# Two transformer blocks on one core: the sums of the norms taken tile by tile beside the products

## The chip, the cores and the metric

The kernel runs on one core of one Trainium2 chip. The metric is the device time of one execution in microseconds. The profile is one execution on the same core, recorded by the hardware profiler.

## The reference

512 tokens of width 2048 in fp32 go through two blocks. The first has a norm, a projection into a pooling half and a state-space half, an output projection and a gate; the second is an attention block with RoPE and 16 heads, and a gated feed-forward of width 5632, both modulated by a vector `c`.

```python
h = rmsnorm(x, norm_gain); proj = h @ w_in            # first block
h = x + concat([ya, yb]) @ w_out
h = h + (p @ w_ple) * sigmoid(h @ w_ple_gate)
x = rmsnorm(h, final_gain)                            # end of the first block

mod = silu(c) @ w_ada + b_ada                         # 6 x 2048 values
h = rmsnorm(x, g_pre_attn) * (1 + sc_a) + sh_a        # a norm of a norm
q, k, v = h @ w_in_2 ...                              # 16 heads
x = x + gt_a * rmsnorm(mix @ w_out_2, g_post_attn)
h = rmsnorm(x, g_pre_ffn) * (1 + sc_f) + sh_f
f = (silu(h @ w_gate) * (h @ w_up)) @ w_down
out = x + gt_f * rmsnorm(f, g_post_ffn)
```

A norm divides each token by the root of its mean square over 2048 channels plus 1e-6.

## The kernel before, in words

**Layout.** Activations lie with channels on the 128 partitions and the 512 tokens along the free axis: 16 tiles (`DT`) of 128x512. A projection is a sequence of *units*: one unit is 128 output channels, a weight of 128x2048 loaded by SyncE into `RAW[slot]`, two slots. fp32 precision comes from a split: ScalarE casts the weight to `WH` (`prep_hi`, L502 to L505), VectorE subtracts to get `WL` (`prep_lo`, L1085 to L1088), the activation is likewise `XH` and `XL`, and TensorE makes three products a tile (L816 to L818), so 48 a unit of 16 tiles. A unit waits for its `WL` (`lo_ready`), for each tile's `XL` (`x_ready`) and for its PSUM bank (`out_read`). The cast of the next weight waits for the unit before it.

**Order.** 32 input units with the scan between them, 8 GLU units, 16 output units (`U_OUT`), 2 of the small projection (`U_PLE`), 16 gate units (`U_PG`), 48 QKV units, three a head (`U_QKV`), 16 units of the second projection (`U_OUT2`), and 11 feed-forward chunks of 8 units gate/up and 4 units down (`U_FFN`).

**The vector c.** `mod` is taken on VectorE beside the output, gate, second projection and last feed-forward units: `ada_chunk` (L1104 to L1110) multiplies 1024 weights a partition with the row `CB` and sums. GpSimd loads the chunks into four slots (L352 to L359). `ada_row` (L687 to L692) on ScalarE waits until the chunks before are used, loads the row `CB` and applies Silu; it then goes on with the casts. `with_ada` (L1119) is VectorE's loop of such a unit: split of the next weight, ada chunks, evacuation.

**A norm** stands between two projections: `squares` on ScalarE (L507 to L510, four times 128x2048), `rms` on VectorE (L1095): four `tensor_reduce` (L1092), four products with a matrix of ones (`ones_sum`, L833 to L837) that put each token's sum on all partitions of PSUM bank 6, the root on ScalarE (L410), the reciprocal on VectorE (L1101), all 128x512. There are six:
- `rms(1)` ahead of the scan (not changed);
- `rms(2)` behind the gate: RES is scaled by it (L1497) and stored as x2; then RoPE's angles and tables and the lambda of the differential heads are computed (L1503 to L1524), and `rms(3)` of the result follows. `modulated` (L1525 to L1538) makes scaled tiles on VectorE, ScalarE adds the shift and casts (`modulated_hi`, L420 to L426), VectorE subtracts;
- `rms(4)` behind the second projection (evacuated to RES, L1667): scale (L1680), add to x2 (L1687), store as x3, `rms(5)` of the sum, `modulated`, and RES is filled with zeros (L1693) ahead of the feed-forward, which adds every chunk's outputs to it (L1727);
- `rms(6)` behind the last chunk, then scale, load of x3, add (L1740) and store (L802).

**Queues.** SyncE issues the weights and the scan's shuffles, GpSimd the ada chunks and spills, ScalarE x, p, `CB`, mask, positions, x2, x3 and the output. `CB`, the ada slots, RoPE's tables and the mask share 48 K to 62 K of each partition, so the tables and the mask come only after the ada chunks.

## Time and profile before

| | us |
|---|---|
| median of 3 runs | 3481.95 (3480.8 to 3482.26) |
| the profiled execution | 3481.74 |
| its span, first to last instruction | 3480.1 |
| TensorE busy | 3241.6 (93%) |
| VectorE busy | 1799.9 (52%) |
| ScalarE busy | 876.2 (25%) |
| TensorE's mean granted clock, 1 is full | 0.96 |

The span in 40 equal slices of 87 us; each digit is tenths:

```profile
PE   8999998999749999999798399999999999999995
DVE  7556565677774445655456823333333333333357
PEclk9999999999869999999699699999999999999997
```

A busy TensorE is not one at its peak: the records overlap, a product of 391 ns begins every 226 ns. "L1092" is a line of the kernel; a releaser in brackets is what ended an idle time.

### The profile page before, as it was taken

To read this page: it belongs to the slowest core of one execution; us is meant where nothing else is said; L and a number is where in the kernel's file an instruction comes from. 1 tells how busy PE (TensorE), PEld (TensorE's weight loads), DVE (VectorE), ACT (ScalarE), POOL (GpSimd) and SP (SyncE) were. 2 spreads that over 40 slices of the span, in tenths; PEclk is the share of its full clock that TensorE was granted. 3 is DMA by queue.
4 is the path that set the end of the run, shared out by engine and by line. 5 is a ranking of instruction groups with operands and counts; after the bars stand their busy time and mean duration, and the time that the engine had idled before them with its cause. 6 is when DMAs were issued, how large, how long until landed. Compare 5 with 4: busy or idle time off the path is not lost.

```text
span 3480.1 us, 37989 instructions
## 1 busy us (share of the span) xinstructions
PE 3241.6 (93%) x14672; PEld 2611.8 (75%) x14672; DVE 1799.9 (52%) x2225; ACT 876.2 (25%) x884; POOL 162.2 (5%) x307
## 2 busy tenths in 40 slices
PE   8999998999749999999798399999999999999995
PEld 6888877888528888887386188888888888888883
DVE  7556565677774445655456823333333333333357
ACT  4323332133332222322312311111111111111121
POOL 1111100111100000000011000000000000000010
PEclk9999999999869999999699699999999999999997
DMA  4443346757512122221265222222222222222263
GB/s 183 129 131 125 120 176 246 265 218 265 184 77 85 73 84 73 85 84 72 108 242 193 89 98 97 96 96 96 96 96 96 94 98 94 93 97 93 96 235 143
DMA packets 87927, 445.88 MB, mean 128 GB/s; under 512 B 18240, under 2 KB 18384, under 8 KB 51504
## 3 DMA queue, kind: packets, MB, share of 16 engines
q1 hardware_dynamic: 50336, 293.89, 23.9%
q0 software_dynamic: 34784, 121.03, 9.7%
q10 hardware_dynamic: 2736, 30.02, 2.1%
q8 instruction: 44, 0.72, 0.1%
q14 instruction: 27, 0.22, 0.0%
HBM read 417.36 MB, written 20.97 MB: 126 GB/s over the span
## 4 chain that ended last, share of the span: by engine, by line
PE 88%; DVE 8%; DMA 1%; ACT 1%; DVEq 1%; issue 1%; ACTq 0%; POOL 0%; SPq 0%; POOLq 0%
PE PS L816 27%; PE PS L818 27%; PE PS L817 27%; DVE SIG L1092 1%; PE PS L999 1%; PE PS L1023 1%; PE PS L1062 1%; DMA CB<-c_row_dram 1%; DVE TMP L1092 1%; DVE PART L1092 1%; DVE RES L1680 1%; DVE WL L1088 1%; DVE XL L1538 1%; PE PS L1014 1%; DVE RSTD L1101 0%
## 5 line engine op out<-in xcount | busy, mean ns | idle before, releaser
L816 PE MATMUL PS<-XH,WH 128*128 128x512 f32 x3488 | 1376.6, 395 | 68.5 <-DVE WL L1088 28.8
L817 PE MATMUL PS<-XL,WH 128*128 128x512 f32 x3488 | 1364.1, 391 | 0.0
L818 PE MATMUL PS<-XH,WL 128*128 128x512 f32 x3488 | 1364.0, 391 | 0.0
L1088 DVE TENSOR_TENSOR WL<-RAW,WH 128x2048 fp32r<-128x2048 f32 x270 | 618.2, 2290 | 588.8 <-ACT WH L505 588.4
L505 ACT ACTIVATE WH<-RAW 128x2048 fp32r<-128x2048 f32 x270 | 516.5, 1914 | 1454.6 <-PE PS L818 1452.4
L816 PEld LDWEIGHTS PS<-XH,WH 128*128 128x128 f32 x3488 | 658.7, 189 | 232.1 <-issue 71.4
L818 PEld LDWEIGHTS PS<-XH,WL 128*128 128x128 f32 x3488 | 658.8, 189 | 138.8
L817 PEld LDWEIGHTS PS<-XL,WH 128*128 128x128 f32 x3488 | 659.5, 189 | 136.0 <-issue 1.9
L816 PE MATMUL PS<-FH,WH 128*128 128x512 f32 x704 | 275.2, 391 | 2.2 <-DVE FL L1720 2.1
L817 PE MATMUL PS<-FL,WH 128*128 128x512 f32 x704 | 274.0, 389 | 0.0
L818 PE MATMUL PS<-FH,WL 128*128 128x512 f32 x704 | 273.9, 389 | 0.0
L1110 DVE CUSTOM_DVE_ANT_0 ADA<-ADA,CB 128x1024 f32<-128x1024 f32 x192 | 224.7, 1221 | 1.3 <-DMA ADA<-w_ada_dram 1.1
L1727 DVE TENSOR_TENSOR RES<-RES,PS 128x512 f32<-128x512 f32 x176 | 120.4, 686 | 199.6 <-PE PS L818 197.8
L359 POOL DMA_DIRECT2D ADA<-w_ada_dram x180 | 95.1, 529 | 1946.7 <-DVE MOD L1110 1679.1
L1716 DVE TENSOR_TENSOR FV<-PS,SIG 128x512 f32<-128x512 f32 x44 | 30.4, 692 | 266.6 <-PE PS L818 266.6
L816 PEld LDWEIGHTS PS<-FH,WH 128*128 128x128 f32 x704 | 132.1, 188 | 33.9 <-DVE FL L1720 6.8
L818 PEld LDWEIGHTS PS<-FH,WL 128*128 128x128 f32 x704 | 132.2, 188 | 27.6
L817 PEld LDWEIGHTS PS<-FL,WH 128*128 128x128 f32 x704 | 132.2, 188 | 27.1
L788 ACT ACTIVATE SIG<-PS 128x512 f32<-128x512 f32 x44 | 26.3, 599 | 382.2 <-PE PS L818 382.2
L837 PE MATMUL PS<-TMP,CON 128*128 128x512 f32 x12 | 11.4, 1049 | 92.9 <-DVE TMP L1092 92.9
L1552 DVE TENSOR_TENSOR TMP<-PS,ROPE 128x512 f32<-128x512 f32 x32 | 22.1, 692 | 121.5 <-PE PS L818 121.4
L837 PEld LDWEIGHTS PS<-TMP,CON 128*128 128x128 f32 x12 | 2.9, 290 | 97.4 <-DVE TMP L1092 97.3
(235 smaller groups left out, 1953.5 us busy)
## 6 DMA issues: line engine op xcount, KB each, us to landing
RAW<-w_units_dram SPq DMA_DIRECT2D x270, 1024.0 KB, 4.8
ADA<-w_ada_dram POOLq DMA_DIRECT2D x192, 512.0 KB, 5.6
BB<-x_dram ACTq DMA_DIRECT2D x2, 4096.0 KB, 12.2
spill_dram<-SIG POOLq DMA_DIRECT2D x24, 256.0 KB, 2.3
XV<-x_t_dram SPq DMA_DIRECT2D x4, 1024.0 KB, 11.0
BB<-x_t_dram ACTq DMA_DIRECT2D x1, 4096.0 KB, 12.3
x_dram<-RES ACTq DMA_DIRECT2D x1, 4096.0 KB, 11.1
x_dram<-BB ACTq DMA_DIRECT2D x1, 4096.0 KB, 12.1
```

Source lines behind the costliest of these rows:

```text
L359: gp.dma_start(ADA[slot][:, :], w_ada[bass.ds(first + ADA_SLOTS * (i + 1) + slot, 1)] .rearrange("a p n -> p (a n)")).then_inc(ada_loaded[ ...
L505: act.activation(WH[:, slot, :], RAW[:, slot, :], ACT.Copy).then_inc(hi_ready, 1)
L816: pe.matmul(PS[:, bank, :], wh, rh[:, x, :], start=k == 0, stop=False)
L817: pe.matmul(PS[:, bank, :], wh, rl[:, x, :], start=False, stop=False)
L818: ins = pe.matmul(PS[:, bank, :], wl, rh[:, x, :], start=False, stop=k == n - 1)
L999: ins = pe.matmul(PS[:, bank, c:c + w], QR[lo:hi, b * P:(b + 1) * P], KR[lo:hi, 0:w], start=True, stop=True, skip_group_check=True)
L1014: ins = pe.transpose(PS[:, TURN_BANK[b], k * P:(k + 1) * P], SMX[:, 0, BLK[b] + k * P:BLK[b] + (k + 1) * P], IDENT)
L1023: ins = pe.matmul(PS[:, 4, b * P:(b + 1) * P], VS[:, k, :], PT[:, c:c + P], start=k == 0, stop=k == b, skip_group_check=True)
L1088: v.tensor_tensor(WL[:, slot, :], RAW[:, slot, :], f32(WH[:, slot, :]), ALU.subtract)\
L1092: v.tensor_reduce(PARTS[c], src[:, 4 * c:4 * c + 4, :].rearrange("p t n -> p n t"), AX.X, ALU.add)\
L1110: v.tensor_tensor_reduce(ADA[slot][:, :], ADA[slot][:, :], CB[:, :], 1.0, 0.0, ALU.mult, ALU.add, (MODH if half else MOD)[:, t:t + 1]).the ...
L1727: v.tensor_tensor(RES[:, 4 * q + m, :], RES[:, 4 * q + m, :], PS[:, m, :], ALU.add).then_inc(out_read, 1)
```

## The change

1. `ada_row` is split in two: the load of `CB` and, later, `ada_silu`. The first load is issued in GLU unit 6, the second behind the last output unit, the third behind the last head's exponentials. The parts of `mod` are cut at 52 instead of 56 and the chunks are shared out differently.
2. RoPE's angles and tables and lambda are computed beside output units 1, 3, 5 and 7, in RES's free tiles, and stored to `rope_dram`; they are loaded with the mask behind the gate.
3. Behind the gate there is one reduction instead of two. Each gate tile is squared by ScalarE when it is final, and VectorE adds it, beside the units, into two sums, plain and weighted with final_gain^2 + eps. The scale of the norm of the norm is the root of (weighted mean + eps^2), so that RES itself stays unscaled; final_gain is folded into the modulation, and RES is scaled to x2 later, beside the second projection, with the row `R1ROW`.
4. The sum over partitions is taken with the squares as weights and a column of ones as the moving operand, so that each token's sum stands in a column [128 tokens, 4]; root and reciprocal run on that. A diagonal matrix times ones puts it back as a row in PSUM bank 7 (or 6), from which VectorE reads it.
5. The second projection is evacuated by ScalarE, scaled by gate and gain, and squared from PSUM; VectorE adds the squares. The next norm's squares are taken tile by tile. The last chunk is treated in the same way, with x3 loaded during it into XH's place; the outputs are stored in five parts.
6. The first two units behind the QKV and the feed-forward norm are interleaved tile by tile (`pair`), the second five tiles behind. RES is no longer filled with zeros: the first chunk copies.
7. ScalarE's loops over output and gate units are written out.

```diff
-ADA_OUT = ADA_PG = [4, 3] * 8
-ADA_OUT2 = [3] * 16
-ADA_FFN = [3, 3, 3, 3, 2, 2] * 2
+ADA_OUT, ADA_PG = [4, 3, 3, 3] * 4, [3, 3, 3, 4] * 4
+ADA_OUT2 = [4, 3] * 8
+ADA_FFN = [4] * 8 + [0] * 4
+LAG = 5
+STORES = [(0, 4), (4, 8), (8, 12), (12, 14), (14, 16)]
...
+        def token_scales(act, n, first=False):
+            act.wait_ge(ms_ready, n)
+            ins = act.activation(RC[:, 0:4], PS[:, 6, 0:4], ACT.Sqrt, bias=CON[:, C_EPS:C_EPS + 1], scale=1.0 / D)
+            if first:
+                ins = act.activation(RC[:, 4:8], PS[:, 6, 4:8], ACT.Sqrt, bias=EPS2, scale=1.0 / D)
+            ins.then_inc(sd_ready, 1)
...
+            for n in range(DT):
+                prep_hi((U_PG + n + 1) // 2, (n + 1) % 2)
+                if n >= 1:
+                    gate_square(n - 1)
+                act.wait_ge(out_done, O_PG + n + 1)
+                act.wait_ge(sig_used, 8 + n + 1)
+                act.activation(SIG[:, n % 2, :], PS[:, n % 2, :], ACT.Sigmoid).then_inc(sig_ready, 1)
+            act.activation(SPARE, ONES[:, 0:1], ACT.Sqrt)
+            gate_square(DT - 1)
+            prep_hi(U_QKV // 2, 1)
+            token_scales(act, 2, first=True)
...
+                act.activation(RES[:, n, :], PS[:, n % 2, :], ACT.Copy, scale=GATE[:, n:n + 1])
+                if n >= 2:
+                    act.wait_ge(acc_done, DT - 1 + n - 1)
+                act.activation(SIG[:, n % 2, :], PS[:, n % 2, :], ACT.Square).then_inc(out_read, 1)
+            prep_hi(U_FFN // 2, 1)
+            token_scales(act, 3)
...
+            def pair(n, o, x0):
+                for u in range(2):
+                    pe.wait_ge(out_read, READ0 + o + u - 1)
+                for k in range(TILES + LAG):
+                    for u, x in ((0, k), (1, k - LAG)):
+                        if not 0 <= x < TILES:
+                            continue
+                        if x == 0:
+                            pe.wait_ge(lo_ready, n + u + 1)
+                        if u == 0:
+                            pe.wait_ge(x_ready, x0 + x + 1)
...
+            def token_sums(src, col, weight, start, stop):
+                for b in range(4):
+                    ins = pe.matmul(PS[:, 6, col + b:col + b + 1], src[:, b * P:(b + 1) * P], weight,
+                                    start=start and b == 0, stop=stop, skip_group_check=True)
+                return ins
+            def token_rows(n, diag, bank):
+                pe.wait_ge(diag_ready, n)
+                pe.matmul(PS[:, bank, :], ONES, diag, start=True, stop=True).then_inc(row_ready, 1)
...
+            token_rows(3, TMP[:, :], 7)
+            for t in range(DT):
+                pe.wait_ge(sq_ready, 4 + DT + t + 1)
+                ins = token_sums(SQ[:, t, :], 0, ONES[:, 0:1], t == 0, t == DT - 1)
+            ins.then_inc(ms_ready, 1)
...
-            def rms(n, src):
+            def token_scales(n, cols=4):
                 v.wait_ge(sd_ready, n)
-                v.reciprocal(RSTD[:, :], RSTD[:, :])
+                v.reciprocal(RC[:, 0:cols], RC[:, 0:cols])
                 v.drain()
+                token_diag(TMP[:, :], cols - 4)
...
+            def gate_square_added(t):
+                v.wait_ge(sq_ready, 4 + t + 1)
...
+                v.tensor_tensor(BB[:, 0, :], BB[:, 0, :], BB[:, t, :], ALU.add)
+                v.scalar_tensor_tensor(out=ACC2[:, :], in0=BB[:, t, :], scalar=GF2[:, t:t + 1], in1=ACC2[:, :],
+                                       op0=ALU.mult, op1=ALU.add).then_inc(acc_done, 1)
...
-            rms(3, SQ)
-            modulated(RES, V_GPRE, DT, BB, 0, X_QKV)
+            token_scales(2, 8)
+            modulated(1, RES, BB, 0, X_QKV, U_QKV + 1)
+            token_diag(SIG[:, 0, :], 0)
...
+            token_scales(3)
+            v.wait_ge(row_ready, 3)
             for c in range(4):
                 sl = slice(4 * c, 4 * c + 4)
-                v.tensor_tensor(BB[:, sl, :], BB[:, sl, :], RES[:, sl, :], ALU.add)
-            v.drain().then_inc(src_ready, 1)
-            v.drain().then_inc(save_go, 1)
-            rms(5, SQ)
-            modulated(BB, V_GPF, 4 * DT, RES, 3 * DT, X_FFN)
-            v.drain()
-            v.memset(RES[:, :, :], 0.0)
+                row_scaled(PS[:, 7, :], sl)
+                v.tensor_tensor(BB[:, sl, :], BB[:, sl, :], RES[:, sl, :], ALU.add).then_inc(x3_ready, 1)
+            prep_lo(U_FFN + 1, 1)
+            token_scales(4)
+            modulated(4, BB, RES, 3 * DT, X_FFN, None)
```

In the first `modulated` the split of the second unit's weight stands between the tiles, behind the fourth scaled tile. `row_scaled` multiplies four tiles by the row in PSUM. The `Sqrt` on `SPARE` loads the root's table ahead of its use.

## Rows read from the trace of the kernel before

**Rows 1.** The page: busy time, share of the span and instructions by engine

```profile
PE 3241.6 (93%) x14672; PEld 2611.8 (75%) x14672; DVE 1799.9 (52%) x2225; ACT 876.2 (25%) x884; POOL 162.2 (5%) x307
```

**Rows 2.** Windows: length, busy (records) of PE, PEld, DVE, ACT, POOL; PEclk, DMA, GB/s

```profile
557.90:565.60 7.70, 0.10 (x1) 0.00 (x0) 2.48 (x2) 4.66 (x3) 0.00 (x0) 0.79 0.20 81
565.60:569.60 4.00, 3.94 (x10) 3.16 (x11) 4.00 (x7) 0.00 (x0) 0.53 (x1) 0.55 0.72 250
928.50:1011.10 82.60, 16.62 (x17) 4.01 (x16) 63.03 (x63) 26.21 (x23) 0.00 (x0) 0.52 0.13 52
1690.00:1700.00 10.00, 10.00 (x13) 3.53 (x12) 8.10 (x12) 3.75 (x6) 0.00 (x0) 0.50 0.00 0
1897.60:1967.80 70.20, 16.62 (x17) 4.04 (x17) 59.18 (x39) 19.26 (x14) 0.00 (x0) 0.52 0.10 45
3431.40:3480.10 48.70, 8.30 (x8) 2.00 (x8) 38.13 (x29) 9.28 (x6) 0.00 (x0) 0.52 0.42 172
```

**Rows 3.** Timeline from gate to QKV: start, us, engine, line, operation, count, idle before

```profile
928.12 0.39 PE L818 MATMUL PS<-XH,WL 128*128 128x512 f32 x1
930.11 0.69 DVE L1489 TENSOR_TENSOR RES<-RES,TMP 128x512 f32<-128x512 f32 x1
936.60 2.08 PE L837 MATMUL PS<-TMP,CON 128*128 128x512 f32 x2 [8.08 <-DVE TMP L1092]
1008.26 2.08 DVE L1533 SCALAR_TENSOR_TENSOR BB<-RES,SM,RSTD 128x512 f32<-128x512 f32 x3
1011.15 0.77 PE L816 MATMUL PS<-XH,WH 128*128 128x512 f32 x1 [7.70 <-DVE XL L1538]
1056.28 0.69 DVE L1632 COPY VT<-PS 128x512 f32<-128x512 f32 x1 [5.80 <-PE PS L818]
```

**Rows 4.** Timeline from the second projection to the third feed-forward unit

```profile
1897.23 0.39 PE L818 MATMUL PS<-XH,WL 128*128 128x512 f32 x1
1964.92 2.08 DVE L1533 SCALAR_TENSOR_TENSOR RES<-BB,SM,RSTD 128x512 f32<-128x512 f32 x3
2011.08 1.92 ACT L505 ACTIVATE WH<-RAW 128x2048 fp32r<-128x2048 f32 x1 [18.10 <-PE PS L818]
```

**Rows 5.** Timeline of VectorE behind the last product

```profile
3431.85 0.17 DVE L1115 TENSOR_TENSOR MOD<-MOD,MODH 128x16 f32<-128x16 f32 x1 [0.19 <-issue]
3465.94 8.90 DVE L1740 TENSOR_TENSOR BB<-BB,RES 128x2048 f32<-128x2048 f32 x4
```

**Rows 6.** Timeline in the second projection: units 1, 9 and 10 (unit's first waits)

```profile
1732.05 0.76 PE L816 MATMUL PS<-XH,WH 128*128 128x512 f32 x1 [7.84 <-DVE WL L1088]
1817.34 2.29 DVE L1088 TENSOR_TENSOR WL<-RAW,WH 128x2048 fp32r<-128x2048 f32 x1 [6.03 <-ACT WH L505]
1821.50 1.92 ACT L505 ACTIVATE WH<-RAW 128x2048 fp32r<-128x2048 f32 x1 [4.19 <-PE PS L818]
1832.38 1.92 ACT L505 ACTIVATE WH<-RAW 128x2048 fp32r<-128x2048 f32 x1 [8.96 <-PE PS L818]
```

**Rows 7.** Groups by form: out<-in, shape, count | busy us, mean ns | idle before

```profile
L885 PE MATMUL PS<-U,GT 128*128 128x64 f32 x128 | 15.1, 271 | 0.0
L885 PEld LDWEIGHTS PS<-U,GT 128*128 128x128 f32 x128 | 15.5, 191 | 0.6
L837 PEld LDWEIGHTS PS<-SIG,CON 128*128 128x128 f32 x24 | 5.8, 291 | 31.6 <-DVE SIG L1092 30.7 <-issue 1.0
L1110 DVE CUSTOM_DVE_ANT_0 ADA<-ADA,CB 128x1024 f32<-128x1024 f32 x192 | 224.7, 1221 | 1.3 <-DMA ADA<-w_ada_dram 1.1
L1533 DVE SCALAR_TENSOR_TENSOR BB<-RES,SM,RSTD 128x512 f32<-128x512 f32 x16 | 11.8, 747 | 0.1
L1658 DVE SCALAR_TENSOR_TENSOR BB<-BB,VEC,PS 128x512 f32<-128x512 f32 x8 | 6.0, 747 | 5.9 <-PE PS L1062 5.9
L498 ACT ACTIVATE SIG<-BB 128x512 f32<-128x512 f32 x16 | 9.9, 627 | 8.1 <-PE PS L1056 5.7 <-DVE BB L1612 2.4
L410 ACT ACT_TABLE_LOAD x5 | 6.4, 1283 | 0.1
```

## What I predict, and how

> **What bounds the kernel now.** I read the page first: TensorE is busy 93% of the span, VectorE 52% [rows 1]. So what can be won is TensorE's idle time, and the 40 slices and the chain of waits put nearly all of it where a norm ends. The windows view prices the stretches [rows 2]; its columns are length, busy time (records) of PE, PEld, DVE, ACT, POOL, the granted clock, DMA. Between the last gate product and the first QKV product lie 82.6 us in which TensorE has 17 records; between the second output projection and the feed-forward 70.2; after the last product 48.7; and 7.7 us ahead of the second output unit, where VectorE and ScalarE wait for the row `CB`. The clock falls to 0.50 (1.2 GHz) in each, and the restart shows it: 10 records in 4.0 us at 0.55, where full speed makes one in 0.2266 us.
>
> **The unit.** One unit of 48 products takes 10.88 us, the distance of two weight casts that wait for it [rows 6], so 0.2266 us a product and 0.68 a tile. VectorE's modulation has two instructions a tile; three first ones take 2.08 us [rows 3], so a pitch of 0.66 us, 1.325 a tile.
>
> **Part 1, the CB row.** It is now loaded during the unit before, so only its Silu, a cast and a split (some 6.5 us after the last GLU tile, at most 10.9 available) stand ahead of the second output unit. Goes: 7.7 us idle, and of the cold restart 4.0 us less 10 x 0.2266 = 1.7, together 9.4. The same at the second projection: 7.84 us idle [rows 6] and 1.7, less the load's issue of some 0.4 us that now stands ahead of the first head square: 9.1. Together **18.5**.
>
> **Part 2, gate to QKV.** Before: last product ends at 928.5, last residual add at 930.8, first modulation at 1008.26, first product 2.9 us later at 1011.1 [rows 2, 3], and the copy of V behind the third unit at 1056.28 [rows 3]. After, step by step from 928.5:
> - The last pass of VectorE is longer: four ada chunks instead of three (1.2 more), the two square additions (1.4), four small operations (0.25 each). These are 3.6 us; the pass used to wait some 1.5 us for the sigmoid, so the residual add ends 2.0 later, at 932.8. The 15 passes before hold 2.3 + 4.9 + 1.4 + 1.5 = 10.1 us at most of 10.88, so they stay covered.
> - ScalarE squares the last tile, 0.63 [rows 7]: 933.5. Its cast of the second QKV weight (1.92) runs beside the sums.
> - 8 sums with the last square, 16 records. No row has a product with one moving column. The nearest is 128x128 weights with 64 columns, records 271 ns long but overlapping: 128 of them are 15.1 us busy, 0.11 to 0.12 each, at full clock; a weight load there takes 191 ns, and 291 at the low clock [rows 7]. The difference, 0.1 us, is what 128 columns cost more at half clock, so I take 0.21 us a record there. I take the low clock here: 3.4 us, 936.9. The first 16 records lie ahead of the square.
> - Two roots on [128, 4] (some 0.25 each with the hand-over), reciprocal 0.2 (a 128x16 operation takes 0.17 [rows 5]), diagonal 0.69: 938.6. One row product at the low clock, 2.08 [rows 3]: 940.8. There the modulation starts: 67.5 us earlier.
> - The pair. First product 2.9 us later. VectorE has 32 steps of 0.66 and the split of the second weight, 2.29: tile 5 at +11.5, the last at +23.4. From tile 5 TensorE has both units: 11 x 1.36 + 5 x 0.68 = 18.3 us. That is slightly slower than VectorE's 1.325 a tile, so TensorE ends it at 940.8 + 11.5 + 18.3 = 970.6. Then the scale row (0.9) and the third unit; its cast and split wait for the first unit's end (966.5) and last 4.2 us, just covered. V at 971.5 + 10.9 = 982.4 against 1056.3: **73.8**.
> - Moved work: RoPE's angles and tables (21 operations on 128x512, each at most the 0.69 of V's copy [rows 3]) go beside output units 1, 3 and 5. Unit 3 gets ten, 6.9 us, and its pass takes 13.5 us, more than a unit, but each is followed by a lighter one, and the split that TensorE needs is first in each pass: no cost as long as that is so. The DMAs on ScalarE's queue (x2 4 MB, mask, RoPE) start at 937 and have 27 us before anybody reads.
>
> **Part 3, second projection to feed-forward.** Before: last product 1897.6, modulation 1964.92, third unit at 2010.9 [rows 4]. After:
> - Scaled copy, square (0.6 each) 1898.9; the weight cast 1.92 stands ahead of the root on ScalarE: 1900.8; root, reciprocal, diagonal 1.5; row 2.08: 1904.3.
> - Four times multiply (2.2), add (2.29), drain: 18.3, so 1922.6. It replaces 16 small multiplies and four adds.
> - The squares follow group by group; the 16 tiles give 128 records. At 0.21 us they take 27.3 us from 1909.9 on and end at 1937.2, later than VectorE. At 0.11 they keep up and end at 1927.1. Which clock TensorE has is the largest open question. The 16-row products between 1690 and 1700 keep it busy all the time and the clock stays at 0.50 [rows 2]; one moving column behind each weight load is nearer to that than to full products. I take 0.21.
> - Root to row 3.4 us: modulation at 1940.6. Pair: tile 5 at +9.3, end at 1968.2. Third unit: cast and split behind CB's load, its Silu and the SiLU of unit 0, some 1.5 us late: 1969.8. Against 2010.9: **41.1** (at 0.11: 51.5). The fill of RES with zeros (6.9 us) goes with it; the first chunk copies instead.
>
> **Part 4, the end.** Last add 3431.7 [rows 5]; square and its addition 0.8, 16 records of which 8 behind the last square (0.9 to 1.7), root to row 3.5: 3438.0. Then 8 operations on four tiles and four on two: 18.6, so 3456.6, where before the last add ends at 3474.8 [rows 5]. The last store is half as large: 5.3 us behind it before, some 4.9 after. **18.6**.
>
> **Part 5, what gets dearer.** Beside unit 7 of the second projection the split waits for CB; it ended at 1819.6, 1.8 us ahead of TensorE's need [rows 6]. Two more ScalarE operations and a later start take 2.5 us: 0.7 lost. The same wait in the last feed-forward chunk now falls at unit 3: 0 to 1.5. Together **-1.5**.
>
> **Sum.** 18.5 + 73.8 + 41.1 + 18.6 - 1.5 = 150.5. The profiled execution took 3481.7 us (span 3480.1 and 1.6 around it), within the three runs' spread round their median 3481.95. So 3331.
>
> **Where the Trainium skill bears on it.** TensorE: Matmul & The Clock Gate, section LDWEIGHTS, gives a load's time by its columns alone, 107 ns for 128, with no second value for the low clock. By that the sums would never lag, which is the first rival; the 291 against 191 ns of rows 7 speak against it. VectorE: DVE Perf Modes, the section on the TRN2 errata, gives an operand in PSUM 120 fixed cycles instead of 58, so an estimate of 65 ns more for each of the 41 operations that now read the row from PSUM, 2.7 us dearer in all. The rows disagree: with the row in PSUM 747 ns, with it in SBUF 747 [rows 7]. I take nothing.
>
> **Rivals.**
> 1. *The sums keep up* (0.25). TensorE takes 0.11 us a record, because loads of 128 rows count as work and the clock rises, or because they don't slow. For it: the loads do fill all 128 rows, unlike those at 1690, and full products bring the clock back in 4 us [rows 2]. 10.4 us less at part 3: 3320.5.
> 2. *Hand-overs are dearer* (0.17). If Square or the scaled copy needs another table than the root, each of three handovers has two table loads more, 6 x 1.28 = 7.7 [rows 7]; and 0.7 us more at each of six chains for small operations that the trace never shows. 3343. Against: behind the head norm's root, copies follow without a load.
> 3. *The clock stays low in a pair* (0.07). Every restart in rows 2 begins at half clock, and the first five tiles feed TensorE only half the time; the clock may come back late or drop once more. A whole pair at 1.2 GHz costs 16 us, both 33: 3347 to 3364.
> 4. *The pairing does nothing* (0.04): the second unit waits for the first, because its split comes late. 7.5 us each: 3346.
> 5. *VectorE becomes the bound* (0.02 in all, 0.01 of it slower than before). In 48 units (output, gate, second projection) it gets more work and every unit waits for its split or evacuation. Now a pass takes 9 to 13.5 us in a unit of 10.88. It costs 48 us for each us over; to eat 150 us the mean pass must reach 14.0 us. Counting instructions gives a mean of no more than 10.5, hence the low chance; at 11.5 it would be 3361.
>
> **How the numbers follow.** Forecast 0.45, the rivals as given. The forecast's own spread is 6 us. The range reaches from the sums that keep up with everything else a little cheaper, 3312, to the dearer hand-overs and one cold pair, 3352; outside lie less than 2 in 10. A difference under 0.2% (7 us) can't be told from none; faster 0.98, same 0.01, slower 0.01.
>
> **What would show it.** The pause from last gate product to first QKV product falls from 82.6 us to about 15; 70.2 becomes two pauses with 128 small records between, whose pitch (0.21 or 0.11) and clock decide rival 1; the tail falls from 48.7 to 30. No idle time of 7.7 us ahead of the second output unit. In the pairs records at 0.2266 and idle only in the first five tiles (rivals 3, 4). Output, gate and second projection: 174 us each, no TensorE idle (rival 5). Table loads between the last square and the root show rival 2. Wrong is the prediction if a chain holds a wait for a DMA, or if the gain goes to places not named here.

## The result, and the profile after

The changed kernel takes 3327.24 us (median of four runs, 3325.46 to 3327.49) where the kernel before takes 3481.38 (3479.53 to 3482.26): a ratio of 0.9557, 95% interval 0.954 to 0.9573. Forecast were 3331.0, with 3312 to 3352 as the range. The profiled execution took 3327.44 us with a span of 3325.8, so 154.3 us less than the span before.

The page of the changed kernel, its busy time by engine and TensorE and its granted clock in the 40 slices:

```profile
PE 3232.4 (97%) x14834; PEld 2634.6 (79%) x14834; DVE 1732.8 (52%) x2233; ACT 871.4 (26%) x948; POOL 162.3 (5%) x307
...
PE   8999999999989999998999999999999999999996
...
PEclk9999999999999999999798899999999999999998
```

TensorE's share of the span rose from 93% [rows 1] to 97% while its busy time hardly changed: the gain is idle time taken away. The slices that were 7 and 4, 3, and 5 in the kernel before are 8, 9 and 6 now. The windows view gives the stretches one by one, in the columns of rows 2: gate's last product to the first QKV product; that pair of units; the last product of the second projection to the first of the feed-forward pair; that pair; and the end.

```profile
918.98:931.40 12.42, 6.07 (x36) 4.36 (x35) 6.29 (x15) 6.97 (x10) 0.00 (x0) 0.72 0.50 211
931.40:958.80 27.40, 25.20 (x97) 19.18 (x98) 23.19 (x31) 11.33 (x14) 0.00 (x0) 0.88 0.42 163
1803.90:1849.60 45.70, 33.35 (x149) 30.01 (x147) 25.20 (x21) 14.19 (x24) 0.44 (x1) 0.55 0.41 159
1849.60:1874.80 25.20, 24.45 (x96) 18.54 (x96) 19.89 (x29) 14.16 (x17) 0.00 (x0) 0.93 0.08 21
3296.70:3325.80 29.10, 4.02 (x19) 2.36 (x18) 20.52 (x14) 1.51 (x3) 0.00 (x0) 0.56 0.35 144
```

82.6 us [rows 2] became 12.4; 70.2 became 45.7, of which TensorE is now busy 33.4, but with small records; 48.7 became 29.1. (The first and third windows open 0.2 us ahead of the last product's end. The last window of rows 2 opens 0.5 us behind it: the last product of the kernel before ends at 3430.94, so its tail is 49.2.) The chain of work behind the gate, from the timeline of the changed kernel (start, length, engine, line, operation, idle before):

```profile
921.43 0.69 DVE L1652 TENSOR_TENSOR RES<-RES,TMP 128x512 f32<-128x512 f32 x1
922.84 1.05 PE L912 MATMUL PS<-CON,BB 128*128 128x1 f32 x8 [1.93 <-ACT BB L749]
923.75 1.14 PE L912 MATMUL PS<-SM,BB 128*128 128x1 f32 x8
924.92 0.26 ACT L428 ACTIVATE SM<-PS,CON 128x4 f32<-128x4 f32 x1 [0.34 <-PE PS L912]
925.38 0.20 DVE L1214 RECIPROCAL SM<-SM 128x8 f32<-128x8 f32 x1 [3.26 <-ACT SM L430]
926.40 2.08 PE L919 MATMUL PS<-TMP,CON 128*128 128x512 f32 x2 [1.51 <-DVE TMP L1208]
928.51 2.06 DVE L1684 SCALAR_TENSOR_TENSOR BB<-RES,SM,PS 128x512 f32<-128x512 f32 x3 [2.17 <-PE PS L919]
931.39 0.76 PE L902 MATMUL PS<-XH,WH 128*128 128x512 f32 x1 [2.91 <-DVE XL L1691]
970.58 0.69 DVE L1794 COPY VT<-PS 128x512 f32<-128x512 f32 x1 [3.41 <-PE PS L865]
```

And the one stretch where TensorE is now late, between the second projection and the feed-forward:

```profile
1808.27 1.80 PE L919 MATMUL PS<-TMP,CON 128*128 128x512 f32 x2 [1.88 <-DVE TMP L1208]
1815.85 27.47 PE L912 MATMUL PS<-CON,SQ 128*128 128x1 f32 x128 [5.79 <-ACT SQ L802]
1828.85 2.19 ACT L802 ACTIVATE SQ<-BB 128x512 f32<-128x512 f32 x4 [2.37 <-DVE BB L1856]
1844.65 2.08 PE L919 MATMUL PS<-TMP,CON 128*128 128x512 f32 x2 [1.33 <-DVE TMP L1208]
1846.77 2.06 DVE L1684 SCALAR_TENSOR_TENSOR RES<-BB,SM,PS 128x512 f32<-128x512 f32 x3 [2.17 <-PE PS L919]
```

ScalarE has squared the last tile at 1831.04, and the 128 one-column records end at 1843.3: TensorE is 12.3 us behind its data.

### The profile page after: what moved, and what is told of

Same layout as the page of the kernel before. It is cut to its first block, busy times and chain, and to the rows that moved or that the text cites. A ratio compares the mean times of both kernels' runs of the same rounds, so it can differ in the third digit from the quotient of the medians.

```text
span 3325.8 us, 38222 instructions
## 1 busy us (share of the span) xinstructions
PE 3232.4 (97%) x14834; PEld 2634.6 (79%) x14834; DVE 1732.8 (52%) x2233; ACT 871.4 (26%) x948; POOL 162.3 (5%) x307
## 4 chain that ended last, share of the span: by engine, by line
PE 92%; DVE 5%; ACT 1%; DMA 1%; issue 1%; DVEq 1%; ACTq 0%; POOL 0%; SPq 0%; POOLq 0%
PE PS L863 28%; PE PS L865 28%; PE PS L864 28%; PE PS L1086 1%; PE PS L1110 1%; PE PS L912 1%; DVE WL L1199 1%; PE PS L1153 1%; ACT WH L519 1%; PE PS L1101 1%; PE PS L983 0%; PE PS L1147 0%; DMA CB<-c_row_dram 0%; PE PS L966 0%; PE PS L930 0%
## 5 line engine op out<-in xcount | busy, mean ns | idle before, releaser
L863 PE MATMUL PS<-XH,WH 128*128 128x512 f32 x3424 | 1344.5, 393 | 21.6 <-DVE XL L1450 14.3
L865 PE MATMUL PS<-XH,WL 128*128 128x512 f32 x3424 | 1334.8, 390 | 0.0
L864 PE MATMUL PS<-XL,WH 128*128 128x512 f32 x3424 | 1334.5, 390 | 0.0
L863 PEld LDWEIGHTS PS<-XH,WH 128*128 128x128 f32 x3424 | 644.1, 188 | 169.3 <-issue 26.9
L865 PEld LDWEIGHTS PS<-XH,WL 128*128 128x128 f32 x3424 | 644.0, 188 | 134.8
L864 PEld LDWEIGHTS PS<-XL,WH 128*128 128x128 f32 x3424 | 644.4, 188 | 134.2 <-issue 2.1
L1901 DVE TENSOR_TENSOR RES<-RES,PS 128x512 f32<-128x512 f32 x160 | 109.8, 686 | 178.4 <-PE PS L865 176.8
L865 PEld LDWEIGHTS PS<-FH,WL 128*128 128x128 f32 x704 | 132.2, 188 | 27.5
L452 ACT ACTIVATE SMX<-SMX,SML 128x128 f32<-128x128 f32 (+1 forms) x96 | 50.5, 550 | 49.5 <-DVE SML L1731 49.5
L1794 DVE COPY VT<-PS 128x512 f32<-128x512 f32 x16 | 11.1, 692 | 96.1 <-PE PS L865 96.1
```

The lines of the kernel that those rows point to most:

```text
L452: ins = act.activation(blk, blk, ACT.Exp, bias=SML[:, 8 + col:9 + col], scale=scale, **kw)
L863: pe.matmul(PS[:, bank, :], wh, rh[:, x, :], start=k == 0, stop=False)
L864: pe.matmul(PS[:, bank, :], wh, rl[:, x, :], start=False, stop=False)
L865: ins = pe.matmul(PS[:, bank, :], wl, rh[:, x, :], start=False, stop=k == n - 1)
L1901: ins = v.tensor_tensor(RES[:, t, :], RES[:, t, :], PS[:, t % 4, :], ALU.add)
```

## The experiments

Twelve kernels were run. Medians are over all executions of a kernel, two to five of them; the kernel before took 3480.4 to 3481.7 us beside them; the differences are to the changed kernel's 3327.24. Nine of them differ from the changed kernel only behind the gate stage, yet its last product ends between 918.5 and 920.9 us in their profiles, and the stretch from the head norm's rows to the first record on the second projection's last square takes between 204.9 us (e3) and 207.8 (the changed kernel). A difference of under 3 us between two totals therefore says little by itself, and the local stretches are read beside it.

### The clock under one-column records

```diff
+            filler(2)
             token_rows(3, TMP[:, :], 7)
+            filler(7)
             for t in range(DT):
                 pe.wait_ge(sq_ready, 4 + DT + t + 1)
```

> The changed kernel with nine idle products added on TensorE ahead of the feed-forward norm (ones times 384 columns of the constants, into a PSUM bank that nobody reads): two while the diagonal for the row is made, seven behind the row until the first squares come. Question: why do the 128 sum records take 0.2147 us each there (27.48 us in all, ending 12.3 us behind the last square), when the groups of 16 beside the other norms take 0.12? Theory A, the clock: it is granted 0.50 in that stretch and 1.00 in the others. Then with TensorE kept busy the records take about 0.12, the sums end about 1 us behind the last square, the row product takes 1.04 instead of 2.08 us, and the kernel takes 12 to 14 us less than the changed kernel: about 3314. Theory B, the records themselves: a run of 128 in a row, each with its own weight load, is paced at 0.21 whatever the clock. Then the stretch keeps its 27.5 us and the kernel its 3327, give or take 1. Theory C: products raise the clock but one-column records let it fall again; then some groups of 32 run at 0.12 and later ones at 0.21, between 3316 and 3324.

It took 3325.42 us (3323.7 to 3327.69), 1.8 less. The windows ahead of the squares, of the first records, and of the rest (columns as in rows 2; the granted clock is the third number from the end):

```profile
1806.40:1814.70 8.30, 6.55 (x20) 3.16 (x18) 6.56 (x5) 1.04 (x4) 0.00 (x0) 1.00 0.32 126
1814.70:1816.00 1.30, 1.30 (x10) 1.30 (x11) 1.23 (x2) 1.30 (x3) 0.00 (x0) 0.84 0.97 403
1816.00:1841.40 25.40, 25.36 (x119) 25.28 (x119) 13.34 (x6) 6.76 (x13) 0.00 (x0) 0.50 0.46 182
```

The idle products did hold the clock at 1.00, and the row product took 1.13 us for 1.80. Then the clock fell with the first records: ten in 1.3 us, and 119 in 25.4, or 0.213 each, at 0.50. TensorE was never idle from the first record on, and its weight loads filled the whole stretch. So the pitch follows the clock (theory A is right on that), a warm start doesn't last, and 25 us of records don't bring the clock back. That is nearest to theory C, only less than it said: not one group of 32 but ten records, so the total is out of its range too.

What made the clock fall is left open. Ahead of its first record TensorE had waited 1.27 us for a square. In e12_rows_lag6, further down, wide products stand where the records stood, and the clock fell there too, just behind a wait of 1.91 us; but it was back 3.4 us later. In e6_rows_warm the same wait of 1.92 us went by at 1.00. A run with idle products up to the very first record would separate the wait from the records; it wasn't made. TensorE's timeline in this kernel, then that of e12_rows_lag6 and two windows of it:

```profile
1814.68 26.68 PE L912 MATMUL PS<-CON,SQ 128*128 128x1 f32 x128 [1.27 <-ACT SQ L802]
```

```profile
1816.13 8.83 PE L1178 MATMUL PS<-SQ,CON 128*128 128x512 f32 x16 [1.91 <-ACT SQ L807]
1816.50:1819.80 3.30, 3.30 (x5) 1.35 (x4) 3.23 (x3) 1.14 (x3) 0.00 (x0) 0.50 0.59 241
1819.90:1824.50 4.60, 4.60 (x12) 1.90 (x10) 4.53 (x3) 2.19 (x4) 0.00 (x0) 1.00 0.55 228
```

> The changed kernel with the sums of the feed-forward norm and of the last norm in the old form: ones as weights, each square as the 512 moving columns, root and reciprocal on the whole row of 128x512, VectorE reads the row from SBUF. e1 showed that one-column records let a full clock fall to half within some 1.5 us. Theory A: wide products bring the clock back, so in the feed-forward norm two tiles take 2.08 us each and the rest 1.04; the sums end at about 1834.6 instead of 1843.3, root and reciprocal take 4.3 us instead of 3.4 for the column chain, and the modulation starts about 8 us earlier. At the last norm the forms are equal within 1 us (5.3 against 5.0 us). Together 7 us less than the changed kernel: 3320. Theory B: the clock stays at half speed under wide products too, as between 1690 and 1700 us before the change: 16 x 2.08 = 33.3 us, 6.7 us later: 3334. By theory C the column form is the better one at the last norm by the whole reciprocal, 3 us, and that offsets part of A: 3322.

```diff
-                ins = token_sums(SQ[:, t, :], 0, ONES[:, 0:1], t == 0, t == DT - 1)
-            ins.then_inc(ms_ready, 1)
-            token_rows(4, TMP[:, :], 7)
+                ins = pe.matmul(PS[:, 6, :], ONES, SQ[:, t, :], start=t == 0, stop=t == DT - 1)
+            ins.then_inc(ms_ready, 1)
...
+            act.activation(R1ROW[:, :], PS[:, 6, :], ACT.Sqrt, bias=CON[:, C_EPS:C_EPS + 1],
+                           scale=1.0 / D).then_inc(sd_ready, 1)
...
+                v.reciprocal(R1ROW[:, :], R1ROW[:, :])
```

3317.91 us (3317.58 to 3318.13), 9.3 less. No idle product was added here. First the windows under the wide products (columns as in rows 2), then VectorE's timeline behind them:

```profile
1815.00:1817.00 2.00, 1.61 (x2) 0.84 (x3) 1.93 (x2) 1.89 (x4) 0.00 (x0) 0.50 0.95 393
...
1821.00:1823.00 2.00, 2.00 (x5) 0.77 (x5) 1.93 (x2) 0.46 (x1) 0.00 (x0) 0.97 0.59 238
```

```profile
1833.53 3.35 DVE L1684 RECIPROCAL R1ROW<-R1ROW 128x512 f32<-128x512 f32 x1 [3.35 <-ACT R1ROW L435]
1836.96 2.07 DVE L1692 SCALAR_TENSOR_TENSOR RES<-BB,SM,R1ROW 128x512 f32<-128x512 f32 x3
```

TensorE starts on the same squares at half clock, and some 6 us later it has 0.97. The sums end at 1832.8, 2.2 us behind the last square; the modulation starts 32.4 us after the first record on the last tile's square of the norm before (1804.60), where the changed kernel needs 41.4 (1805.34 to 1846.77): 9.1 us, though the long reciprocal is in it. At the last norm, where the column form has 16 records, it is the better one: from the last square addition to the first scaling 6.99 us in this kernel, 6.14 in the changed one. Theory A in both places; theory C's 3 us for the reciprocal is 0.85.

> Row sums in the feed-forward norm alone, and idle products (ones times 384 columns, about 0.78 us each at full clock) wherever TensorE waits in the three chains: two and one around the gate norm's sums and three behind its row, two and six ahead of the feed-forward norm's squares and eight behind its sums, one at the last norm. Theory A, the clock is the cost: the feed-forward norm's sums keep up with the squares and end about 1 us behind the last, its modulation starts 11 us earlier; each of the three row products takes 1.04 instead of 2.08 us; some more from a pair that starts at full clock: 13 to 15 us less than the changed kernel, 3312 to 3314. Theory B, idle products stand in the way of the real ones and give back what they bring at the gate and last norms: 11 us less: 3316. Theory C: the pairs are bound by VectorE's modulation and gain nothing from a warm start: the upper end of A.

```diff
             token_sums(ACC2, 4, ONES[:, 0:1], False, False)
+            filler(2)
...
+            filler(1)
             token_rows(1, TMP[:, :], 7)
+            filler(3)
...
+            filler(2)
             token_rows(3, TMP[:, :], 7)
+            filler(6)
...
+                ins = pe.matmul(PS[:, 6, :], ONES, SQ[:, t, :], start=t == 0, stop=t == DT - 1)
             ins.then_inc(ms_ready, 1)
+            filler(8)
...
+            filler(1)
             token_rows(5, TMP[:, :], 7)
```

3314.04 us (3313.65 to 3314.64), 13.2 less than the changed kernel and the fastest of all: 0.9519 of the kernel before, interval 0.9503 to 0.9535. Some 10 us of that belong to the edit: from the second projection's last product to the third feed-forward unit it is 61.6 us for 71.6. Another 2.3 lie in the attention and the second projection (V's copy to the last product, 831.2 us for 833.5), where the two kernels are the same. TensorE's timeline, a line of the gate norm and two of the feed-forward norm:

```profile
925.65 2.07 PE L924 MATMUL PS<-TMP,CON 128*128 128x512 f32 x2 [0.37 <-DVE TMP L1223]
...
1812.17 3.70 PE L1181 MATMUL PS<-SQ,CON 128*128 128x512 f32 x8 [1.92 <-ACT SQ L807]
1816.73 3.70 PE L1181 MATMUL PS<-SQ,CON 128*128 128x512 f32 x8 [0.86 <-ACT SQ L807]
```

With the clock held, each of the four groups of four tiles takes the same 3.70 us and waits for ScalarE. At the gate norm the idle products brought nothing that can be told from the spread: between them stand 16 one-column records, and behind those the row product still took 2.07 us, at half clock. From the first record on the last square to V's copy that kernel needs 47.7 us, the changed kernel 47.7 as well, and three others without idle products there 48.7 (e8), 49.0 (e5) and 49.4 (e1). At the last norm the row product took 2.08 us too, and the tail is 29.3 us for 29.1. So of theory A's three row products one got the full clock. The feed-forward pair, from its first product to the third unit's, took 26.0 us from a full clock (1836.63 to 1862.65) and 26.0 from half (1849.64 to 1875.64): VectorE's modulation bounds its beginning, as theory C had it.

### What each part is worth

> The changed kernel with the squares of the gate stage taken late: ScalarE squares all 16 tiles and VectorE adds them only behind the last gate unit, all else as changed. What taking the sums beside the products is worth, apart from their form. Theory A: nearly the whole gain of the gate part is this placement; VectorE's 15 pairs of additions at 1.43 us each (21.5 us) and the first 24 sum records at the low clock come on the path: 23 to 26 us more than the changed kernel, 3350 to 3353. Theory B: the additions overlap ScalarE's squares and the placement is worth only the 16 squares at 0.55 us, so 8 to 10 us more: 3336. Theory C: VectorE was late in the gate stage and that stage gets shorter; then less than 20 us and the gate units come closer together.

```diff
-                if n >= 1:
-                    gate_square(n - 1)
...
+            for t in range(DT):
+                gate_square(t)
...
+            for n in range(1, DT):
+                v.drain()
+                gate_square_added(n - 1)
```

3349.44 us (3348.37 to 3349.95), 22.2 more. ScalarE had its 16 squares in 8.4 us, but VectorE's additions (its first is at 921.6, the last ends at 942.4) held the records (timelines of ScalarE, VectorE and TensorE):

```profile
920.98 8.41 ACT L749 ACTIVATE BB<-RES 128x512 f32<-128x512 f32 x16
942.41 1.87 PE L911 MATMUL PS<-CON,BB 128*128 128x1 f32 x8 [23.49 <-DVE ACC L1660]
953.02 2.06 DVE L1684 SCALAR_TENSOR_TENSOR BB<-RES,SM,PS 128x512 f32<-128x512 f32 x3 [2.17 <-PE PS L918]
```

The modulation starts 24.5 us later than in the changed kernel: theory A, with a total just below its range. A third of the gate part's gain is this placement.

> The changed kernel with the first block's norm not folded in: behind the row of the gate norm VectorE scales RES (four groups of 2.3 us), ScalarE squares the scaled tiles, TensorE takes 128 sum records again, and a second root, diagonal and row stand ahead of the modulation. (The copy of RES that the second projection reads back is then scaled once too often; nothing else differs.) What is the folding worth by itself? Theory A, sums at the half clock: they start 3 us behind the row (928.5 + 2.9) and take 27.5 us, root to row 3.4: modulation at 962.3 instead of 928.5, 34 us more than the changed kernel, 3361. Theory B, the sums keep up with the squares at 0.12 us: last square at 939.9, modulation at 944.5: 16 us more, 3343. Theory C: part of it is hidden by the loads that the attention waits for: under 10 us.

```diff
             token_scales(2, 8)
+            v.wait_ge(row_ready, 1)
+            for c in range(4):
+                v.tensor_tensor(RES[:, 4 * c:4 * c + 4, :], RES[:, 4 * c:4 * c + 4, :],
+                                PS[:, 7, :].unsqueeze(1).broadcast_to([P, 4, S]), ALU.mult).then_inc(z1, 1)
...
+            v.wait_ge(z6, 1)
             modulated(1, RES, BB, 0, X_QKV, U_QKV + 1)
```

3362.65 us (two runs, 3362.24 and 3363.07), 35.4 more, theory A (34). Only the time of this kernel is of use, since RES is scaled once too often in it. VectorE's scaling and TensorE's records in the timeline:

```profile
930.69 8.88 DVE L1712 TENSOR_TENSOR RES<-RES,PS 128x2048 f32<-128x2048 f32 x4 [2.17 <-PE PS L926]
933.69 27.46 PE L919 MATMUL PS<-CON,SQ 128*128 128x1 f32 x128 [3.04 <-ACT SQ L765]
```

That is the largest part of the change among those that a run took back, and 27.5 us of it is again the 128 records at half clock. VectorE's scaling and ScalarE's squares are over at 941.8, so with row sums at full clock it would cost about 16 us by estimate; that wasn't run.

> The changed kernel with the two units behind both norms one after the other instead of interleaved; the second one's weights are still split early. The first unit then ends with VectorE's last modulated tile, the second 10.9 us later. Theory A, order alone: 4.9 us later at the first norm (pair now ends at 958.8, would at 963.7) and 4.7 us at the second: 9 to 10 us more than the changed kernel, 3336 to 3337. Theory B, the clock: with TensorE fed only every 1.33 us the clock falls during the first unit or at the start of the second, as it did at 1033 us in the kernel before: another 2 to 8 us, 3339 to 3345. Theory C: interleaving does nothing, 3327.

```diff
-                for k in range(TILES + LAG):
-                    for u, x in ((0, k), (1, k - LAG)):
+                for k in range(2 * TILES):
+                    for u, x in ((0, k), (1, k - TILES)):
```

3335.25 us (3334.73 to 3337.29), 8.0 more. From the pair's first product to the start of V's turning it is 45.1 us for 39.9 (5.2 more), and from the feed-forward pair's first product to the end of the span 4.8 more: theory A's two prices. Together that is 10.0; the profiled executions lie 9.9 us apart, the medians 8.0. The clock was back to 1.00 in the middle of the lone first unit and stayed there, against theory B (windows, columns as in rows 2):

```profile
941.00:946.00 5.00, 4.58 (x14) 2.54 (x12) 5.00 (x9) 2.62 (x5) 0.00 (x0) 0.79 0.91 378
946.00:952.00 6.00, 4.24 (x14) 2.24 (x14) 6.00 (x10) 3.32 (x5) 0.00 (x0) 1.00 0.01 3
```

> The changed kernel with the loads of the row CB ahead of the output and the second projection issued as in the kernel before, directly ahead of their Silu. Theory A (my part 1): both stalls come back whole, 9.4 and 9.1 us with their cold restarts: 18 us more than the changed kernel, 3345. Theory B: at the second projection VectorE and ScalarE have other work by then and only the first comes back: 3336. Theory C: the load was hidden anyway: 3327.

```diff
-                    ada_row(0)
...
-            ada_row(2)
...
+            ada_row(0)
             ada_silu(0)
...
+            ada_row(2)
             ada_silu(2)
```

3349.02 us (3346.57 to 3350.01), 21.8 more: theory A, dearer than its 18. Both stalls are back in TensorE's timeline:

```profile
567.41 0.77 PE L863 MATMUL PS<-XH,WH 128*128 128x512 f32 x1 [9.38 <-DVE WL L1199]
1659.58 0.77 PE L863 MATMUL PS<-XH,WH 128*128 128x512 f32 x1 [7.83 <-DVE WL L1199]
```

The second is the 7.84 us of rows 6; the first was 7.7 before [rows 2]; it is longer now, and two loads (positions and lambda's vectors) are issued ahead of it that were not there before; whether they are the reason wasn't tried.

> The changed kernel without the three small square roots that load ScalarE's table ahead of time. Theory A: each of the three chains then has one table load of 1.28 us between the sums and the root: 3.8 us more than the changed kernel, 3331. Theory B: the squares or the scaled copies need other tables too, so loads come between them as well, more than 5 us more. Theory C: ScalarE waits long enough for the sums that the load is hidden anyway: no change.

3329.58 us (3329.18 to 3329.95), 2.3 more, between theories A and C. ScalarE loads one table in each chain, and only ahead of the root; none stands between square, copy and scaled copy (timelines of ScalarE and TensorE at the gate norm, then a line of ScalarE's at the feed-forward norm and one at the last):

```profile
923.92 0.63 ACT L749 ACTIVATE BB<-RES 128x512 f32<-128x512 f32 x1 [2.34 <-DVE RES L1648]
925.74 1.84 PE L908 MATMUL PS<-SM,BB 128*128 128x1 f32 x8
926.37 1.28 ACT L428 ACT_TABLE_LOAD   x1
...
1807.84 1.28 ACT L428 ACT_TABLE_LOAD   x1
...
3302.51 0.26 ACT L428 ACTIVATE SM<-PS,CON 128x4 f32<-128x4 f32 x1 [0.91 <-PE PS L908]
```

From the last square to the root it is 3.73 us there and 2.77 in the changed kernel, 3.70 for 2.27 ahead of the feed-forward, 3.45 for 2.79 at the end. Only the middle one, 1.4 us, is the load's. At the gate norm the load ends at 927.65 and TensorE's last record at 927.58, so it is hidden; the 16 records took 3.0 us there for 2.0, because less of them ran at full clock. At the end the root waits 0.91 us for TensorE behind the load.

### What covers the moved work, and the lag

> The changed kernel with eight more additions of 128x424 on VectorE beside each of the 16 output units (about 0.65 to 0.7 us each with its drain, 5.4 us a unit), which nobody reads. VectorE is busy 6.9 us of 10.88 in a plain unit of that stage and 8.7 in one with RoPE work, so it has 2 to 4 us to spare. Theory A: VectorE becomes the bound, each unit takes what its pass takes: (7.6 + 5.4 - 10.88) x 16 = 34 us, less some 8 us that the early split gives as slack: 26 to 34 us more than the changed kernel. Theory B: the work is hidden by what TensorE has queued: under 5 us more. Theory C: the additions cost more than their time, since the ada chunks' buffers come free later and their loads too: over 40 us more.

```diff
             def beside_out(n):
+                for _ in range(8):
+                    tt(R1ROW[:, 0:424], CON[:, 0:424], CON[:, 0:424], ALU.add)
```

3369.56 us, 42.3 more, all of it in that stage (the same wait of a PLE product that lies at 744.80 lies at 787.06). VectorE is the bound there now, 46.1 of 50 us busy and TensorE 41.4, as theory A says. The number is theory C's, over 40, but not its reason: VectorE waits for no load of a chunk there. What theory A's 34 us left out are the restarts at half clock behind TensorE's waits of 5 to 6 us (a first record of 0.77 us, where behind a wait of 0.70 at 703.43 it is 0.47), and a wait of 10.15 us behind the last output unit, in which VectorE makes its ada chunks and the eight additions ahead of the small projection's `XL`. A window of the stage, and two of these waits:

```profile
600.00:650.00 50.00, 41.44 (x172) 33.47 (x171) 46.14 (x75) 8.27 (x7) 5.82 (x11) 0.93 0.60 224
```

```profile
614.65 0.77 PE L863 MATMUL PS<-XH,WH 128*128 128x512 f32 x1 [5.79 <-DVE WL L1199]
761.20 0.77 PE L863 MATMUL PS<-XH,WH 128*128 128x512 f32 x1 [10.15 <-DVE XL L1588]
```

In the changed kernel TensorE is busy all 50 us of the same stretch: RoPE's 21 operations cost nothing there because VectorE had the room.

> The changed kernel with LAG 3 instead of 5: the second unit of each pair follows three tiles behind. Theory A: the pair is bound by TensorE from the moment the second unit starts; starting it two tiles earlier fills the waits of the first tiles (0.3 us and less each, 0.7 us in all at each norm): 0.5 to 1.5 us less than the changed kernel, 3326. Theory B: the second unit's weights are not split in time at the gate norm and TensorE waits for them: 1 to 3 us more. Theory C: no difference.

```diff
-LAG = 5
+LAG = 3
```

3327.98 us (3327.15 to 3330.34): no difference, theory C. Two waits of 0.3 us are gone, one in each pair, and a longer one stands behind the feed-forward pair: the third unit's split, which begins when the first unit frees its weights, has less lag to hide in (TensorE's timeline):

```profile
1877.01 0.50 PE L863 MATMUL PS<-XH,WH 128*128 128x512 f32 x1 [2.17 <-DVE WL L1199]
```

In the changed kernel that wait is 0.81. Behind the gate pair there is one of 0.83 now, where the changed kernel has none.

> Row sums in the feed-forward norm and idle products in the chains (3314.0 in its run) together with LAG 3. Theory A: the pair starts at full clock at the feed-forward norm, TensorE waits 0.36 us at each of its first five tiles for VectorE there, and LAG 3 takes two of these waits: 0.7 us less, and the gate pair as in the kernel with LAG 3 alone: 3312.5 to 3313.5. Theory B: the end of the pair is set by VectorE's last tile: no change.

The edits of e6_rows_warm and of e10_lag3 together.

3317.79 us (3315.59 to 3318.89), 3.8 more than with LAG 5: neither theory. The same 2.17 us wait is there, and behind it the clock fell, so that ten products took 3.4 us instead of 2.3. From the third unit to the last chunk's wait for CB that is 2.0 us more than in the kernel with LAG 5; the second projection, where the two don't differ, took 2.3 us more. The wait, and the window behind it:

```profile
1864.31 0.50 PE L868 MATMUL PS<-XH,WH 128*128 128x512 f32 x1 [2.17 <-DVE WL L1214]
```

```profile
1865.00:1868.40 3.40, 3.40 (x10) 2.68 (x9) 3.22 (x4) 0.00 (x0) 0.00 (x0) 0.52 0.78 299
```

> Row sums in the feed-forward norm with the idle products around it (two, six and eight), none at the gate and last norms, and LAG 6. With LAG 3 the third unit waited 2.17 us for its split behind the feed-forward pair and the clock fell to half for 3.4 us; with LAG 5 it waited 0.81 us without that. Theory A, the lag is what covers the third unit's cast and split: each tile more of lag adds 0.68 us of cover and at most 0.36 us to the pair; the wait falls to 0.1 to 0.5 us, the sum is within 0.5 us of the kernel with LAG 5 and idle products (3314.0), and leaving the idle products at the other two norms out costs nothing: 3313.5 to 3314.5. Theory B: the idle products at the gate norm were worth their 1 us of warm start: 3315 to 3316.

```diff
             token_sums(ACC2, 4, ONES[:, 0:1], False, False)
-            filler(2)
...
-            filler(1)
             token_rows(1, TMP[:, :], 7)
-            filler(3)
...
-            filler(1)
             token_rows(5, TMP[:, :], 7)
...
-LAG = 5
+LAG = 6
```

That diff is against e6_rows_warm. 3317.92 us (3316.91 to 3318.23), 3.9 more than that kernel: outside both theories. The lag did what theory A says: no wait is left behind the feed-forward pair, and from its first product to the last chunk's wait for CB it is 1370.3 us for 1370.2, so LAG 5 and 6 are equal. The fall of the clock at its first sums (shown at e1) cost nothing, since the sums wait for the squares later on: from the second projection's last product to the pair it is 35.6 us in e6, e11 and e12. At the gate norm, from the first record on the last square to V's copy, it is 48.6 us for e6's 47.7; kernels without idle products there lie between 47.7 and 49.4, so that doesn't decide for theory B. The rest lies where the two kernels don't differ: the gate stage ends 1.8 us later (a 0.67 us wait at 580.56 is new) and the second projection takes 1.9 us more, of which 0.7 is its wait for the third row of CB (1.15 for 0.43). Why these loads land later in one kernel than in another I can't say.

## Why the prediction was right, point by point

The parts, forecast and measured, in us of gain; each measured one is the difference of the same two events in both traces:

| part | from, to; before and after | forecast | measured |
|---|---|---|---|
| 1, first row of CB | start to the last gate product: 928.5, 919.2 | 9.4 | 9.3 |
| 2, gate to QKV | from there to V's copy: 127.8, 51.4 | 73.8 | 76.4 |
| 1 and 5, the second projection | to its last product: 841.3, 833.5 | 8.4 | 7.8 |
| 3, the norms behind it | to the third feed-forward unit: 113.3, 71.6 | 41.1 | 41.7 |
| 5, feed-forward | to the last product: 1420.1, 1421.1 | -0.8 | -1.0 |
| 4, the end | to the end of the span: 49.2, 29.1 | 18.6 | 20.1 |
| sum | | 150.5 | 154.3 |

**Part 1 and 5** held, stalls and prices; e4 brings them back. The wait that part 5 put at 0.7 us for the second projection is 1.5, and the one of the last chunk 0.65.

**Part 2** is 2.6 us better. Two terms were mis-sized, by 1.3 us each. One is "I take the low clock here": behind the last gate product the clock was still 1.00, and 0.91 while the last 16 records ran, which took 2.0 us instead of 3.4. The other is VectorE's last pass, which ended 3.0 us behind the last product instead of 4.3. So the modulation starts 9.3 us after the last product instead of 12.3. The pair and the third unit took 42.1 us, forecast 41.6. That clock is luck: in e5, e9 and e10 the same 16 records, in the same chain, took 2.9 to 3.6 us. Runs took back some 65 us of this part, if their differences may be added: the placement beside the units (e2, 24.5), the folding (e9, 35.4) and the pair (e3, 5.2). The other 11, RoPE's work among them, stand on the traces alone.

**Part 3**, the largest open question, came out as put: 128 records in 27.47 us for 27.3, the clock 0.50, the pair's end 70.8 us behind the last product for 70.6. Rival 1 was wrong about the place it was made for, and right for the groups of 16 at full clock: 0.11 us a record there. The low clock was forecast from products of 16 rows, the nearest row there was. The runs bear it out for one-column records themselves: in no kernel with 128 of them did they bring the clock back, and e1, which had it at 1.00 just ahead of them, lost it. No run took back the rest of this part or part 4, 57 us beside the pair; for them the stretches in the traces are the evidence. The section on LDWEIGHTS in TensorE: Matmul & The Clock Gate of the Trainium skill gives a load's time as its columns divided by 1.2, so 107 ns for 128, and no second value for the low clock. At full clock a record every 0.11 us is near that; at half clock the loads took 0.33 us each and a record came every 0.21, which it doesn't have.

**Part 4** is 1.5 better: 19.0 us of operations for 18.6, but the last store ends 3.1 us behind the last addition, not 4.9.

**Rival 2** (dearer hand-overs): no table is loaded between square and root, and without the preloads one of three loads is on the path, 1.4 us (e8). **Rival 3**: the clock is 1.00 between 3 and 10 us into a pair and stays there to its end in the changed kernel and in e3. It can drop once more, as the rival said: in e6 it was 0.50 for 3.4 us in the gate pair, behind a wait of 2.5 us, and with LAG 3 behind the feed-forward pair. **Rival 4**: the pairing is worth 5 us at each norm, where 7.5 was said. **Rival 5**: with some 5 us more of VectorE work a unit the output stage is bound by VectorE and costs 42 us more (e7); the changed kernel has 3 to 4 us a unit to spare there (VectorE is busy 34.6 and 30.1 of 50 us) and 2 in the gate stage (95.4 of 118.9).

What the forecast did not ask is whether the column form was the right one. It is by 0.85 us where 16 records do, and it costs 9 us where 128 are needed (e5); with the idle products at that norm the change left some 10 us behind (e6).

## What to carry to other kernels

Where TensorE does the sum of a norm and its data come tile by tile, price each form of the sum at the clock that it gets. Here 128 one-column products ran at half clock in every kernel that had them, behind nine idle products all but the first ten, while wide ones brought the clock back within 6 us as they did the same sum. Take sums beside the products they follow, fold one norm's scale into the next one's sum, and interleave the first two units behind a norm with a lag that still covers the third unit's cast and split. When two variants differ by less than the stages they share vary between kernels (here 3 us), compare the stretch, not the total.

## What the hardware showed that was not expected

- One-column records don't bring a low clock back, though TensorE is never idle and its weight loads fill the time: 0.50 over 25 us in e1 and over all 27.5 us in the changed kernel. In e1 a full clock fell within 1.3 us of their start (0.84 in the first 1.3 us), behind a wait of 1.27; whether the records or the wait did it is not shown. The groups of 16 in the changed kernel ran at 1.00 (0.11 us a record), all but the last one behind the gate, which ran at 0.91.
- A wait of 2.17 us behind a full-speed pair was followed by ten products at 0.52 in e11, and by a clock of 0.61 over 3 us in e10, while one of 0.81 us in e6 was followed by none. The length of the wait alone doesn't decide: behind waits of 1.92 and 1.91 us ahead of the feed-forward norm's first sums the clock fell in e11 and e12, and stayed at 1.00 in e6.
- With the row in PSUM VectorE's modulation takes 741 ns a tile, with it in SBUF 741 in e5 and 747 before [rows 7]; an operand in PSUM costs nothing here. The section on the TRN2 errata of VectorE: DVE Perf Modes in the Trainium skill has 120 fixed cycles for it instead of 58; the measurement decides.
